# A recurrent gate without its reciprocal, another order of the projections, and stores issued from another queue

## The reference

```python
q, k, v, rx, rg, ga, gb = jnp.split(h @ w_in[l], SPLIT_POINTS, axis=-1)
attn = band attention over q, k, v            # 8 heads of 64, 640 keys for 128 queries, learned bias
xc, cr_new = causal_dwconv(rx, cr_prev, rnn_conv_w[l], rnn_conv_b[l])      # width 4
r = sigmoid(blockdiag(xc, wa) + ba);  ig = sigmoid(blockdiag(xc, wx) + bx)
log_a = -8 * r * softplus(-lam);      a = exp(log_a)
u = sqrt(-expm1(2 * log_a)) * (ig * xc)
h[t] = a[t] * h[t-1] + u[t]                    # scan along the rows
rnn = h * gelu(rg)
merged = sigmoid(ga) * (attn @ w_branch[:512]) + sigmoid(gb) * (rnn @ w_branch[512:])
x = x + gate * (merged @ w_out)
```

## Time and profile before

| | |
|---|---|
| median of the runs | 3095.0 us |
| the profiled execution's own time | 3099.6 us |
| its span | 3097.8 us |
| busy: PE, DVE, ACT | 2857.5 us (92%), 1592.1 us (51%), 1077.1 us (35%) |
| rounds: first projection matmul of rounds 0 to 3 | 94.5, 333.0, 558.7, 783.9 us |
| last attention store issued | 1006.2 us |

### The profile page before, as it was taken

One profiled execution on the slowest core, in us unless ns is written; L12 is line 12 of the kernel. 1 busy time (PEld: TensorE's weight loads), 2 busy tenths in 40 slices (PEclk: granted clock), 3 DMA queues, 4 the chain that ended last, 5 costly groups with the idle time before them and its releaser, 6 DMA issues.

```text
span 3097.8 us, 52735 instructions
## 1 busy us (share of the span) xinstructions
PE 2857.5 (92%) x20144; PEld 1823.9 (59%) x20144; DVE 1592.1 (51%) x2765; ACT 1077.1 (35%) x1973; POOL 49.4 (2%) x37
## 2 busy tenths in 40 slices
PE   6797988979978799999979899999999999999998
PEld 3356557457457344444479766666666666666665
DVE  3665365266275233344367776776666666211112
ACT  4335235235245111111135555454444444100000
POOL 0000000000000000000001110000000000000000
PEclk9898998999989899999989999999999999999999
DMA  7100100110110522112165311111111115522211
GB/s 271 37 15 30 44 18 26 44 36 8 44 36 0 201 89 82 68 61 68 68 161 141 99 55 55 55 55 55 57 65 57 55 55 204 166 89 81 80 57 38
DMA packets 168519, 226.68 MB, mean 73 GB/s; under 512 B 49408, under 2 KB 126720, under 8 KB 165840
## 3 DMA queue, kind: packets, MB, share of 16 engines
q1 hardware_dynamic: 152000, 202.49, 19.9%
q10 hardware_dynamic: 15328, 19.77, 1.9%
q0 software_dynamic: 1072, 2.65, 0.2%
HBM read 164.00 MB, written 63.50 MB: 73 GB/s over the span
## 4 chain that ended last, share of the span: by engine, by line
PE 77%; DVE 11%; issue 4%; ACT 4%; DMA 1%; ACTq 1%; DVEq 0%; SPq 0%
PE ps L2090 43%; PE ps L2063 16%; PE ps L1904 9%; PE ps L1981 3%; PE ps L1968 2%; DVE arena L1390 2%; DVE arena L1621 1%; ACT arena L943 1%; PE ps L1955 1%; PE ps L1923 1%; PE ps L1866 1%; DMA arena<-mixer_outputs 1%; DVE arena L1353 1%; ACT arena L828 1%; DVE arena L1282 1%
## 5 line engine op out<-in xcount | busy, mean ns | idle before, releaser
L2090 PE MATMUL ps<-arena 128*128 128x352 f16 (+1 forms) x11016 | 1489.7, 298 | 31.2 <-DVE arena L1541 16.4
L2090 PEld LDWEIGHTS ps<-arena 128*128 128x128 f16 x11016 | 1026.4, 97 | 493.5 <-issue 19.1
L2063 PE MATMUL ps<-arena 128*128 128x512 f16 (+1 forms) x2880 | 519.6, 343 | 24.0 <-DVE arena L1509 13.0
L2063 PEld LDWEIGHTS ps<-arena 128*128 128x128 f16 x2880 | 241.7, 97 | 302.0 <-issue 19.5
L1904 PE MATMUL ps<-arena 128*128 128x512 f16 (+1 forms) x1920 | 355.6, 348 | 30.1 <-DVE arena L1282 19.2
L1904 PEld LDWEIGHTS ps<-arena 128*128 128x128 f16 x1920 | 163.6, 99 | 222.4 <-issue 37.6
L1801 DVE SCALAR_TENSOR_TENSOR arena<-ps,arena 128x352 f32<-128x352 f32 (+1 forms) x64 | 30.0, 491 | 352.3 <-PE ps L2090 302.8
L1520 DVE SCALAR_TENSOR_TENSOR arena<-ps,arena 128x512 f32<-128x512 f32 (+1 forms) x80 | 47.6, 599 | 302.5 <-PE ps L2063 300.1
L1003 ACT ACTIVATE arena<-ps 128x352 f32<-128x352 f32 x264 | 119.8, 464 | 199.1 <-PE ps L2090 199.1
L1628 DVE SCALAR_TENSOR_TENSOR arena<-arena 128x512 f16<-128x512 f32 x154 | 103.7, 688 | 128.2 <-ACT arena L967 128.2
L1179 ACT ACTIVATE arena<-arena 128x352 f32<-128x352 f32 x48 | 23.9, 498 | 408.7 <-DVE arena L1801 408.7
(11 more groups left out here) (187 smaller groups left out, 2526.1 us busy)
## 6 DMA issues: line engine op xcount, KB each, us to landing
arena<-in_w_up SPq DMA_DIRECT2D x44, 512.0 KB, 4.0
ffn_hidden<-arena SPq DMA_DIRECT2D x44, 512.0 KB, 3.2
arena<-in_w_in SPq DMA_DIRECT2D x38, 512.0 KB, 5.1
arena<-ffn_hidden SPq DMA_DIRECT2D x5, 3872.0 KB, 19.7
arena<-in_w_mod_rest SPq DMA_DIRECT2D x32, 512.0 KB, 3.3
arena<-in_w_down SPq DMA_DIRECT2D x7, 1408.0 KB, 6.5
arena<-mixer_outputs SPq DMA_DIRECT2D x8, 1056.0 KB, 16.6
arena<-in_x_cols SPq DMA_DIRECT2D x12, 704.0 KB, 4.6
```

Source lines behind the costliest of these rows:

```text
L2063: mm = pe.matmul(out, wt[:, wp, k, :], act_t[:, k, hp, t:t + w], start=(k == k0 and m == 0), stop=(k == k1 - 1 and m == 2))
L2090: mm = pe.matmul(out, wt[:, k, wp, :], act_t[:, k, hp], start=(first and k == 0 and n == 0), stop=(last and k == K - 1 and n == 2), skip_g ...
```

## The change

It has four parts.

1. Since tanh(x) = (1 - a^2)/(1 + a^2) with a = exp(-x), DVE now computes 1 - a^2 as tanh(x)(1 + a^2): a square (`tensor_tensor`) and one `scalar_tensor_tensor`. The add and the reciprocal are gone. The chain on DVE has 9 steps instead of 10; its second step is followed at once by ig times xc.
2. The projections come in the order rx, q, gates, rg, k, v. ACT's work follows: q's copies, then the sigmoids, tanh and exp, then the gelu, then the root, then k. On DVE the whole gate chain up to the product with the gelu now stands ahead of k, the split of v's weights inside it, and all five `v_out` at the end.
3. The stores of k, `rstage`, v and of the attention output are issued by SP, behind its loads of the round, the last one behind a wait for the end of the attention.
4. Of the two weight splits at p == 3, the second moves to p == 4.

```diff
-        UNITS = [(WRX, 0), (WRG, 1), (WQ, 0), (WK, 1), (WV, 0)]
+        UNITS = [(WRX, 0), (WQ, 1), (WRG, 0), (WK, 1), (WV, 0)]
...
-        USES = (["A"] * 5 + ["A"] * 5 + ["V"] * 5 + ["A"] * 10 + ["V"] * 5 + ["V"] + ["V"] * 5)
+        USES = (["A"] * 5 + ["V"] * 5 + ["A"] * 10 + ["A"] * 5 + ["V"] * 5 + ["V"] + ["V"] * 5)
...
-        U_RX, U_RG, U_Q, U_G, U_K, U_KC, U_V = 0, 5, 10, 15, 25, 30, 31
+        U_RX, U_Q, U_G, U_RG, U_K, U_KC, U_V = 0, 5, 10, 20, 25, 30, 31
...
+                sp.wait_ge(kf_ready, 2 * j + 2)
+                sp.dma_start(a["k_prompt"][ds(j, 1)].rearrange("j p t -> (j p) t"), kf[:, 0:PAST])\
+                    .then_inc(kf_stored, 16)
...
+                sp.wait_ge(rg_dve, 9 * j + 9)
+                sp.dma_start(mix_d[ds(j + NJ, 1), :, :, 0:TP].rearrange("j p s t -> (j p) s t"),
+                             rstage[:, :, 0:TP]).then_inc(rnn_stored, 16)
...
+                sp.wait_ge(c_dve, NV * j + 2 * NV)
+                sp.dma_start(a["v_prompt"][:, :, ds(j, 1), :].rearrange("c p j d -> p (c j) d"),
+                             vv[:, NT - 4:NT, :]).then_inc(v_stored, 16)
...
+                sp.wait_ge(ot_ready, (NT + 1) * (j + 2))
+                sp.dma_start(mix_d[ds(j, 1)].rearrange("j p s t -> (j p) s t"), ost).then_inc(attn_stored, 16)
...
+                act.wait_ge(rg_dve, 9 * j + 2)
+                act.activation(bufT[:, 0:LB], bufA[:, 0:LB], ACT.Tanh).then_inc(rg_act, 1)
+                act.activation(bufA[:, 0:LB], bufA[:, 0:LB], ACT.Exp, scale=-1.0).then_inc(rg_act, 1)
...
+                split_hi(4, 0, 3 * j + 3, NU * j + NU + U_RG + 5)
+                act.wait_ge(rg_dve, 9 * j + 5)
+                act.activation(bufT[:, 0:LB], bufT[:, 0:LB], ACT.Sqrt).then_inc(rg_act, 1)
...
                     if p == 3:
                         split_hi(0, 0, 3 * j + 4, NU * j + 2 * NU)
+                    if p == 4:
                         split_hi(1, 1, 2 * j + 3, NU * j + 30 + NU)
...
-                step(dve.tensor_scalar(bufR, bufT, 1.0, None, ALU.add))
-                after(3)
-                step(dve.reciprocal(bufR, bufR))
+                step(dve.tensor_tensor(bufR, bufA[:, 0:LB], bufA[:, 0:LB], ALU.mult))
                 after(4)
-                step(dve.scalar_tensor_tensor(bufT, bufT, 2.0, bufR, ALU.mult, ALU.mult))
...
+                step(dve.scalar_tensor_tensor(bufT, bufR, 1.0, bufT, ALU.add, ALU.mult))
+                split_lo(5 * j + 5, 0)
                 dve.wait_ge(rg_act, 6 * j + 5)
+                step(dve.tensor_tensor(bufI, bufI, bufT, ALU.mult))
...
+                for n in range(2, 6):
+                    k_lo(n)
+                dve.wait_ge(v_stored, 32 * j + 32)
+                for n in range(5):
+                    v_out(n)
```

More of the change, by code:

```diff
@@ L749, in _ @@
                 for n, (t, w) in enumerate(BLOCKS):
[L750 to L753, removed]
-                for n, (t, w) in enumerate(BLOCKS):
                     src = filled(U_Q + n)
@@ L766, in _ @@
                                        bias=gbias[:, g:g + 1]).then_inc(c_act, 1)
+                act.wait_ge(rg_dve, 9 * j + 2)
+                act.activation(bufT[:, 0:LB], bufA[:, 0:LB], ACT.Tanh).then_inc(rg_act, 1)
+                act.activation(bufA[:, 0:LB], bufA[:, 0:LB], ACT.Exp, scale=-1.0).then_inc(rg_act, 1)
+                for n, (t, w) in enumerate(BLOCKS):
+                    o = 0 if t < TP else 3
+                    act.activation(bufG[:, t + o:t + o + w], filled(U_RG + n)[:, 0:w], ACT.Gelu_apprx_tanh,
+                                   scale=CS).then_inc(c_act, 1)
+                split_hi(4, 0, 3 * j + 3, NU * j + NU + U_RG + 5)
+                act.wait_ge(rg_dve, 9 * j + 5)
+                act.activation(bufT[:, 0:LB], bufT[:, 0:LB], ACT.Sqrt).then_inc(rg_act, 1)
                 def k_hi(n):
@@ L1331, in _ @@
                 split_lo(5 * j + 3, 0)
-                split_lo(5 * j + 4, 1)
                 def q_lo(n):
@@ L1376, in _ @@
                     q_lo(n)
-                split_lo(5 * j + 5, 0)
-                dve.wait_ge(c_act, NA * j + NA + 20)
+                split_lo(5 * j + 4, 1)
+                dve.wait_ge(c_act, NA * j + NA + 15)
                 step(dve.memset(bufA[:, TP:TP + 3], 0.0))
@@ L1407, in _ @@
                                             col("h0", 0, 4)[:, ds(j, 1)], ALU.mult, ALU.add))
-                v_out(1)
-                after(8)
+                after(7)
                 dve.tensor_copy(holdv[:, ds(j, 1), 6:7].rearrange("p j c -> p (j c)"), bufX[:, TP - 1:TP])
@@ L1413, in _ @@
                 dve.wait_ge(held, j + 1)
+                dve.wait_ge(c_act, NA * j + NA + 20)
                 step(dve.tensor_tensor(bufX, bufX, bufG, ALU.mult))
-                v_out(2)
+                k_lo(0)
+                k_lo(1)
                 dve.wait_ge(rg_act, 6 * j + 6)
-                after(9)
+                after(8)
                 step(dve.scalar_tensor_tensor(rstage[:, 1, :], bufX, XS, rstage[:, 0, :], ALU.mult, ALU.subtract))
-                v_out(3)
-                v_out(4)
+                for n in range(2, 6):
+                    k_lo(n)
+                dve.wait_ge(v_stored, 32 * j + 32)
+                for n in range(5):
+                    v_out(n)
                 dve.wait_ge(aux_loaded, 16 * j + 16)
@@ L1924, in _ @@
                             .then_inc(c_filled, 1)
+                pe.wait_ge(w_split, 5 * j + 8)
+                unit(U_RG, 0)
                 pe.wait_ge(w_split, 5 * j + 9)
```

57 lines of the change are left out of this document (14 added, 43 removed).

## The result

The changed kernel takes 3025.8 us (median of four runs, 3025.37 to 3027.43), the kernel before beside it 3096.1 (four runs, 3094.53 to 3100.21): a ratio of 0.977, 95% interval 0.976 to 0.979, or 70.3 us less. The forecast was 3026. The profiled execution took 3025.8, its span is 3024.0, which is 73.8 shorter than before; its mean granted clock is 0.974.

A forecast was written before the change was run, and what follows sets the result against it. PE was taken as the bound, with 77% of the path. Four rounds at -17.4 us give -69.6, the end +0.7: -68.9, so 3026 against the median of 3095.0; own range 3018 to 3034 (0.60).

The forecast's parts named there:

- The wait of 13.3 for the last copy of v: PE's wait before the attention's first scores: shrinks to some 0.4, gain 12.9 us a round, bounds 12.5 and 13.3.
- Most of the gain is the order: Gate chain on DVE: the square gives back 2.4 us, but reordering brings the chain's start forward from 75 to 53.5.
- 13 to 14 us in hand: Projections: DVE ends its k copies at about 105 us into the round, PE ends v at 118.7.
- The rival of a wait that stays in part: Last copy of v: a chain 20 us longer leaves 6 us a round, 3050; range 3040 to 3085, chance 0.10.
- The first exp: Attention's start: first exp 0.8 us after the first scores instead of 4.5, gain 3.7 a round, bounds 3.6 and 3.9.
- The clock: Attention's opening: PE comes straight from v at a higher clock, gain 1.2 us a round, bounds 0 and 1.9.
- The splits apart: Weight splits in the attention at p == 3 and p == 4: +0.4 us a round, bounds -1.2 and +1.1.
- The end: Behind the last round: SP issues the store before loading the merge's weights, +0.7 us, bounds 0 and 3.
- The sum: Whole kernel: -17.4 us a round, -69.6 over four rounds, end +0.7, together -68.9.
- stall inside the projections: PE in the projections: a bank drained late would look like the wait staying in part; no new wait was expected.
- late tile: Next round's third weight tile: landing at 60 us stops ACT, then PE's banks, 42 us slower, 3137; slower had chance 0.02.
- the cover of 18 us: SP's loads for the next round: needed 23 us into it, landing 5.1 us after issue, so a delay of 3.4 disappears.

The follow-up runs named there:

- e2: The changed kernel with the old add, reciprocal and product put back in place of the square: 3027.2 us, ratio 0.977 to the kernel before.
- e11: The changed kernel with a second reciprocal of 13.4 us, its result unused, ahead of the scan on DVE: 3032.3 us, ratio 0.979 to the kernel before.
- e12: The kernel before with only the stores moved, all issued by SP, order and arithmetic as before: 3080.9 us, ratio 0.994 to the kernel before.
- e3: The changed kernel with the stores of k, rstage and v back on ACT: 3037.4 us, ratio 0.981 to the kernel before.
- e10: The kernel before with unused matmuls on PE: 54 in the wait for v's last copy, 16 behind the first scores: 3097.6 us, ratio 1.000.
- a0: The changed kernel run once more, unaltered, with the third group of experiments: 3026.6 us, ratio 0.977 to the kernel before.
- e5: The changed kernel with both weight splits at p == 3 again: 3025.9 us, ratio 0.977 to the kernel before.
- e4: The changed kernel with only the attention output's store back on ACT: 3027.3 us, ratio 0.977 to the kernel before.
- e8: The changed kernel with PE's four rounds written out, the other engines' loops kept: 3014.4 us, ratio 0.973 to the kernel before.
- e9: The kernel of e8 with both weight splits for the next round moved out of the attention, beside PE's v: 2990.3 us, ratio 0.965 to the kernel before.
- e6: The kernel before with 54 unused matmuls on PE during its wait for the last copy of v: 3098.1 us, ratio 1.000 to the kernel before.

## Why the prediction was right, step by step

- **The wait of 13.3 for the last copy of v** (predicted -12.9 a round): the projections are shorter by 12.9, 13.2, 12.9 and 12.9, and the wait is 0.4, the number given. Right in mechanism and size. "Most of the gain is the order" was too careful: once the order is changed, the arithmetic adds nothing (e2). The add was priced at 2.4 and takes 1.26, which changes nothing in the sum.
- **13 to 14 us in hand**: the profile has k's last copy done at 418.27, which is 103.8 into the round for the forecast's 105, and v done on PE at 432.80, 14.5 later. e11 makes it 12 by the time, since v's copies are queued too. So the step is right to 1 or 2 us. The rival of a wait that stays in part, which was to decide from 13 us on, begins a little earlier: one reciprocal more, and PE waits 1.1 us longer a round.
- **The first exp** (-3.7): 3.6 to 3.7. e12 confirms the price by itself, 3.6 with no other edit. The prediction put it down to the stores on SP; e3 shows that the new order alone would have brought half of it.
- **The clock** (-1.2, bounds 0 to 1.9): the opening is 0.9, 0.6, 0.6 and 0.6 shorter. The clock did rise, from 0.71 to 1.00, but PE's work of 6.63 busy us fell only to 5.74, and the steps there are tied to ACT, whose 4.92 us are the same in both windows. This term was mis-sized by a factor of two: 0.6, and by e10 about 0.3 net. The Trainium skill (TensorE: Matmul & The Clock Gate, A second HAM failure mode: psum-queue depth-cycling) tells of a kernel in which frequent short idles between groups of matmuls keep moving the clock between its two levels. The opening's 1.00 here and in e10 is against that for this stretch. In the next one, where a split holds ACT and DVE, the clock is down for part of the time (0.76), though not in round 0 of a0.
- **The splits apart** (+0.4, bounds -1.2 to 1.1): the stretch with the first split is 0.1 to 0.2 shorter in rounds 1 to 3, and e5 gives nothing for moving the second back. Wrong in sign, within its bounds. PE's waits for the bias step did fall, from 12.1 to 8.4 us, and it gained nothing.
- **The end** (+0.7, bounds 0 to 3): 3.3 less in the profiles, outside the bounds. This is the step that failed. I priced only what SP must do before its loads, and not that the loads stood in the way of the store: on ACT's queue the store was issued beside SP's weight loads, now it goes ahead of them. SP must wait for the landing of the store before it loads c and the mixer outputs, and this wait is what became shorter: from the end of the attention to the load of c it is 6.0 us for 7.3. That is 1.3 of the 3.3, and every profile has it. The other 2.0 lie between the load of c and the first matmul on the mixer outputs, 27.0 for 29.0. There the kernels differ by themselves, 26.9 to 27.6 in the seven with the store on SP and 27.2 to 29.8 in the five with it on ACT, and no run takes this part apart. e4, which moves this store alone, shows 2.0 of the 3.3 in the profile and nothing in the median.
- **The sum**: rounds 70.4 for 69.6, end +3.3 for -0.7, together 73.7 in the profile for 68.9. In the medians it is 70.3. So the gain was forecast 1.4 us too small by the medians, and 4.8 by the profiles: the profiled execution of before lay 3.5 us above the median beside it, that of after 0.1 below its own. That 3026 itself was met to 0.2 us is in part luck: the forecast counted from a median of 3095.0, and with the fourth run it was 3096.1. A clock priced too high, an end priced too low and the 1.5 us of round 0 also went into the same sum.
- **Rivals**: no stall inside the projections, and no late tile, though SP issued the loads after the attention's end; the cover of 18 us was not needed.

What stays open: why the end of the attention to the mixer outputs takes 34.2 and 34.4 in e8 and e9, with the store on SP, for 33.0 (the store lands as fast there, and the difference lies behind the load of c: 28.2 and 28.4 for 27.0); and why PE's start of a round is slow in rounds 1 and 2 of e8, but not in round 3.

## What to carry to other kernels

When the bound engine waits for the last short operation of another, look at the queue in front of it: moving the long chain to where that engine rests took away 52 us of waiting, and made an operation five times cheaper inside the chain worthless. Parts of a change that remove the same wait don't add up (the arithmetic alone 39, everything but the arithmetic 71, all together 70 to 73), so measure each alone and each left out. Where loads wait for a store to land, look at what goes beside it: ahead of the weight loads this one landed 1.4 us sooner. After such a move the slack is a resource: 12 us beside v were enough to take the weight splits out of the attention, for another 24 us.

## What the runs showed of the hardware that was not expected

- A turn of PE's loop costs 3.2 to 3.4 us; with the rounds written out it costs 0.05 to 0.06 (e8). The prediction took it as given.
- PE's granted clock fell within the 4.5 us between the first scores and the first exp, in which PE was busy for 0.79, although it had been kept busy nearly up to there (e6); with that stretch filled it stayed at the upper level (e10).
- The clock can be worth nothing: a stretch whose pace other engines set took 14.07 us at 0.76 and at 1.00 (a0).
- exp's table load takes 1.28 us, and the exp follows 0.01 us later (438.44 and 439.73 in e3): nothing else is to be paid for the change of table there. It is the same right behind other work: tanh ends at 420.42 in the kernel before, the load takes 1.28, and the next exp starts at 421.73.
- On DVE, over 128x2115 in f32, the square costs 2.36 us, like the other passes with two tensor operands here, and the add of a constant 1.26; the reciprocal costs 13.38, 5.7 times the square.
